# Two-layer streaming encoder: the body of the expert loop holds four experts in place of two

## What is computed

```
def swiglu(h, wg, wu, wd):
    return (jax.nn.silu(h @ wg) * (h @ wu)) @ wd
...
    logits = (h @ p['router'][j]).astype(jnp.float32)
    top_v, top_i = lax.top_k(logits, TOP_K)
    gates = jax.nn.softmax(top_v, axis=-1)
    w_e = jnp.einsum('btk,btke->bte', gates, jax.nn.one_hot(top_i, N_EXPERTS, dtype=jnp.float32))
    for e in range(N_EXPERTS):
        out = out + w_e[..., e:e + 1] * swiglu(h, p['e_gate'][j, e], p['e_up'][j, e], p['e_down'][j, e]).astype(jnp.float32)
```

## Time and profile before

| | |
|---|---|
| median of 3 runs | 2176.72 us (2172.87 to 2177.47) |
| the profiled execution: time | 2173.31 us |
| the profiled execution: span of the trace | 2171.5 us |
| PE busy | 2080.8 us (96%) |
| DVE busy | 1413.3 us (65%) |
| ACT busy | 1021.1 us (47%) |
| granted PE clock, mean | 0.97 |
| expert stage | about 1100 us to the end |

### The profile page before, as it was taken

How to read it: one execution, slowest core, us unless ns; L and a number is a source line. 1 busy time by engine, 2 the same in 40 slices (tenths; PEclk the granted TensorE clock), 3 DMA queues, 4 the chain that set the end, 5 groups by cost and what they waited for, 6 DMA issues and landing times.

```text
span 2171.5 us, 27716 instructions
## 1 busy us (share of the span) xinstructions
PE 2080.8 (96%) x10564; PEld 1688.0 (78%) x10564; DVE 1413.3 (65%) x1736; ACT 1021.1 (47%) x1168; POOL 140.4 (6%) x108
## 2 busy tenths in 40 slices
PE   7999998899999999997899999999999999999998
PEld 5767685699997777785778888888887888888886
DVE  1445633377772447433368787978878788797887
ACT  1333311143332334211256666766666666676765
POOL 2000000154430000000000000000000000000000
PEclk9999998999999999998889999999999999999999
DMA  7312210424443322110469897988979889898895
GB/s 278 123 64 117 88 48 17 161 101 162 174 161 119 120 106 88 59 59 17 154 227 341 320 343 299 360 321 336 344 268 356 322 335 344 305 353 327 330 349 214
DMA packets 61584, 467.41 MB, mean 215 GB/s; under 512 B 7592, under 2 KB 7848, under 8 KB 9744
## 3 DMA queue, kind: packets, MB, share of 16 engines
q1 hardware_dynamic: 58896, 459.86, 56.0%
q0 software_dynamic: 2560, 5.85, 0.8%
HBM read 462.66 MB, written 3.02 MB: 214 GB/s over the span
## 4 chain that ended last, share of the span: by engine, by line
PE 92%; DVE 5%; ACT 2%; issue 1%; POOL 0%; DMA 0%; DVEq 0%; ACTq 0%; POOLq 0%
PE ps L501 12%; PE ps L946 10%; PE ps L951 10%; PE ps L948 9%; PE ps L646 8%; PE ps L971 5%; PE ps L977 5%; PE ps L972 5%; PE ps L922 4%; PE ps L665 3%; PE ps L842 2%; PE ps L846 2%; PE ps L849 2%; PE ps L959 1%; PE ps L865 1%; PE ps L866 1%
## 5 line engine op out<-in xcount | busy, mean ns | idle before, releaser
L1871 DVE TENSOR_TENSOR ring_r<-ring,unit_hi 128x2048 fp32r<-128x2048 f32 x288 | 653.0, 2290 | 134.2 <-ACT unit_hi L1355 131.9
L1355 ACT ACTIVATE unit_hi<-ring 128x2048 fp32r<-128x2048 f32 x288 | 542.6, 1913 | 3.4 <-issue 3.4
L946 PE MATMUL ps<-unit_hi,hg_hi 128*128 128x512 f32 x896 | 251.2, 402 | 2.3 <-issue 2.3
L948 PE MATMUL ps<-unit_hi,hg_lo 128*128 128x512 f32 x896 | 242.2, 392 | 0.0
L646 PE MATMUL ps<-h,ring 128*128 128x288 f32 x768 | 217.8, 423 | 1.7 <-ACT arena L1188 1.0
L501 PE MATMUL ps<-h,ring 128*128 128x288 f32 x832 | 208.6, 413 | 9.5 <-DVE h L1463 9.5
L951 PE MATMUL ps<-ring_r,hg_hi 128*128 128x512 f32 x772 | 212.3, 397 | 1.4 <-issue 1.4
L501 PEld LDWEIGHTS ps<-h,ring 128*128 128x128 f32 x832 | 160.4, 193 | 56.1 <-issue 11.4
L948 PEld LDWEIGHTS ps<-unit_hi,hg_lo 128*128 128x128 f32 x896 | 169.3, 189 | 37.2
L946 PEld LDWEIGHTS ps<-unit_hi,hg_hi 128*128 128x128 f32 x896 | 160.7, 189 | 34.2 <-issue 2.8
L971 PE MATMUL ps<-unit_hi,h_e_hi 128*128 128x512 f32 x448 | 178.2, 398 | 3.2 <-DVE h_e_lo L1886 3.2
(11 more groups left out here) (383 smaller groups left out, 2889.1 us busy)
## 6 DMA issues: line engine op xcount, KB each, us to landing
ring<-in_w_exp SPq DMA_DIRECT2D x288, 1024.0 KB, 4.8
ring<-in_w_mix SPq DMA_DIRECT2D x44, 1536.0 KB, 6.6
unit<-in_w_exp SPq DMA_DIRECT2D x48, 1024.0 KB, 4.8
ring<-in_w_ffn SPq DMA_DIRECT2D x22, 1536.0 KB, 6.3
rel_table<-rel_row POOLq DMA_DIRECT2D x8, 256.0 KB, 8.9
const<-in_const SPq DMA_DIRECT2D x1, 1186.0 KB, 8.6
x<-in_xT SPq DMA_DIRECT2D x1, 1152.0 KB, 5.1
out_yT<-x SPq DMA_DIRECT2D x4, 288.0 KB, 2.2
```

Of the source, the lines that this page charges most:

```text
L946: mm(out, hg_hi[:, hp, 4 * w + k, :], hi[:, 512 * k:512 * k + 512], start=(w == 0 and k == 0), stop=False)
L948: mm(out, hg_lo[:, hp, 4 * w + k, :], hi[:, 512 * k:512 * k + 512], start=False, stop=False)
L1355: fn(unit_hi(q), unit(q), ACT.Copy).then_inc(s["uhi_made"], 1)
L1871: v.tensor_tensor(unit_lo(q), unit(q), unit_hi(q).bitcast(F32), ALU.subtract).then_inc(s["ulo_made"], 1)
```

## The change

On PE, ACT and DVE the loop advances by two, and its body holds `it2` and `then2 = it2 + 1`, four experts. `final - 1` is even for all three values of `final`, so the loop covers the same numbers: 1 to 2, 1 to 6 or 1 to 10. SP, POOL, the data and the order of the work are as they were.

```
-                with pe.Fori(1, final) as it2:
+                with pe.Fori(1, pe.snap(final - 1), 2) as it2:
                     expert(it2, 0, False, False)
                     expert(it2, 1, False, False)
+                    then2 = pe.snap(it2 + 1)
+                    expert(then2, 0, False, False)
+                    expert(then2, 1, False, False)
                 expert(final, 0, False, False)
                 expert(final, 1, False, True)
```

More of the change, by code:

```diff
@@ L1406, in experts @@
                 final = act.value_load(npass[0:1, 1:2], min_val=3, max_val=11)
-                with act.Fori(1, final) as it2:
+                with act.Fori(1, act.snap(final - 1), 2) as it2:
                     expert(it2, 0, False, False)
                     expert(it2, 1, False, False)
+                    then2 = act.snap(it2 + 1)
+                    expert(then2, 0, False, False)
+                    expert(then2, 1, False, False)
                 expert(final, 0, False, False)
@@ L1940, in experts @@
                 final = dve.value_load(npass[0:1, 1:2], min_val=3, max_val=11)
-                with dve.Fori(1, final) as it2:
+                with dve.Fori(1, dve.snap(final - 1), 2) as it2:
                     expert(it2, 0, False, False)
                     expert(it2, 1, False, False)
+                    then2 = dve.snap(it2 + 1)
+                    expert(then2, 0, False, False)
+                    expert(then2, 1, False, False)
                 expert(final, 0, False, False)
```

## The result

| | before | the change |
|---|---|---|
| median | 2177.98 us (6 runs, 2172.87 to 2179.73) | 2168.36 us (6 runs, 2163.38 to 2170.01) |
| ratio | | 0.9956, 95% interval 0.9942 to 0.9970 |
| profiled execution: time, span | 2173.31, 2171.5 us | 2169.02, 2167.2 us |
| PE's instruction packets (q8), all | 80 | 78 |

The change is faster by 0.44% (0.30 to 0.58%), 9.6 us between the medians. The predicted 2171.2 us is 2.8 us too high, and the gain at 5.48 us too small by the medians. A second measurement of the same kernel (experiment 6) gave 0.9954 (0.9942 to 0.9966).

A forecast was written before the change was run, and what follows sets the result against it. PE was taken to bound the kernel, stalled only at its one expert-loop back-edge: -5.48 us there, 0 for the new branch, SP's loads and longer body, so 2176.72 - 5.48 = 2171.2 us, range 2166.5 to 2175.0.

The forecast's parts named there:

- What bounds, and where: Expert stage: PE, 96% busy, sets the end; its only idle times, 2.3 and 1.4 us, lie at the back-edge.
- The price: PE's back-edge between experts 3 and 4: removing it frees 5.48 us, from select distances 138.65 and 133.17.
- the forecast's own median: Whole kernel: 2171.2 us, from before's median 2176.72 less 5.48, carrying over 3.4 us between median and profiled execution.
- ACT and DVE: Their back-edges must go too; with PE's alone removed, PE would wait about 4.7 us for DVE's `h_e_lo`, queued behind ACT.
- the forecast of 4.7: Near the back-edge: PE's wait in us for `h_e_lo` if PE alone lost its stall, 5.48 less 0.76 spare.
- SP and the loads: SP keeps its loop; its loads still arrive in time, cost 0, thinnest spare 1.0 us, units behind gaining on ACT.
- Rival B: At SP's loads: PE's stall hid them, so ACT would wait without it; 2173 to 2175 us, chance 0.07.
- The longer body: Four-expert loop body: the same instructions pass each engine but for the branch, so it costs 0 us.
- Rival C: New code of the longer body: refills stop PE, 8 x 1.42 = 11.4 less 5.48, +5.9 us, 2182.6; chance 0.05.
- Rival A: At the back-edge: it isn't what costs, or the stall only moves; no change, 2176.7 us, chance 0.11.
- its smaller version: At the back-edge: second issue wait and slow clock hang on something else, only 2.32 us goes; 2174.4 us.

The follow-up runs named there:

- experiment 6: The changed kernel, unedited, measured once more; ratio 0.9954 (0.9942 to 0.9966) to before, median 2168.57 us.
- experiment 11: The kernel before, unedited, run a third time for its trace; ratio 1.0000 (0.9990 to 1.0009).
- experiment 2: Kernel before with four experts in PE's loop body alone, ACT and DVE keeping two; ratio 0.9992 (0.9981 to 1.0003) to before.
- experiment 10: Kernel before with four experts in PE's and ACT's loop bodies, DVE keeping two; ratio 0.9993 (0.9983 to 1.0002) to before.
- experiment 3: Kernel before with four experts in ACT's and DVE's loop bodies, PE keeping two; ratio 1.0004 (0.9993 to 1.0016) to before.
- experiment 4: The changed kernel with SP's loop over pairs of experts written out too; ratio 0.9964 (0.9951 to 0.9977) to before, median 2167.66 us.
- experiment 5: Kernel before with the loop turned by one expert on PE, ACT and DVE, giving two back-edges; ratio 0.9973 (0.9963 to 0.9983) to before.
- experiment 1: The kernel before, unedited, run once more; ratio 1.0002 (0.9993 to 1.0011), 9.31 us for the back-edge.
- experiment 7: Kernel of experiment 3 with PE's code shifted by 48 wait instructions at the start; ratio 0.9977 (0.9967 to 0.9987) to before.
- experiment 8: Kernel of experiment 3 with PE's code shifted by 128 wait instructions at the start; ratio 1.0009 (1.0000 to 1.0019) to before.
- experiment 9: Kernel before, its back-edge kept on PE, ACT and DVE, with SP's loop written out; ratio 0.9989 (0.9979 to 0.9999) to before.

## Why the prediction was right, and where it was off

**What bounds, and where.** Right. The only PE waits of the stage were those of the back-edge, and with it gone there are none: every distance is 133.1 to 133.2 us in the change, twice.

**The price.** This step was mis-sized. The term was 5.48 us, "because it is measured over a whole expert". It is, but in one execution, and the price varies: 5.48 in the first trace, 9.31 and 9.33 in the two others, with q8 fetching two pieces at once (1637.00 and 1637.13 in experiment 11) and a granted clock of 0.57 in 1640 to 1652 us in both, where the first trace had 0.86. The 105 runs of before and twelve of the change put the gain at 8.0 us by the medians and 8.8 by the means. An estimate from 5.5 and 9.3 makes 66% of the executions the dear kind by the medians and 87% by the means; two traces of three were. That there are just two values isn't shown: the runs of before spread from 2172 to 2180 us without a gap. That the direction held doesn't hang on this, as the cheap form already gains 5.5 us. Which form the one trace read had was chance: with 9.31 us the same sum would have given 2167.4. The same may show in the forecast's own median: the 3.4 us by which the profiled execution lay below the median were carried over as a constant, but the two executions of the dear kind took 3.1 and 2.5 us more than it (2176.38 and 2175.83 against 2173.31). So for the most part they may have been this price, and would then go with the back-edge. Taking the profiled time as the base, with its own price, would have given 2167.8, nearer to the 2168.4 measured.

**ACT and DVE.** Right that PE alone gains nothing (5.9 us remain, experiment 2; the forecast of 4.7 lacked the half clock after the wait). The reading of DVE was incomplete: the prediction saw it as queued behind ACT, and experiment 10 shows a refill of its own, worth 5.1 us. Each of those tested costs most of it by itself, 5.7 for PE (3), 5.9 for ACT with DVE (2), 5.1 for DVE (10), and together 5.5 to 9.3; ACT alone wasn't run. PE's 5.7 is from a trace with a lone packet; a dear form of it, as in experiment 1, isn't ruled out. They overlap, so they can't be added, and neither PE's alone (2), nor ACT's and DVE's (3), nor PE's and ACT's (10) was worth removing without the rest.

**SP and the loads.** Right in that it costs nothing. SP's pause stays, from 1620.22 to 1628.20 in the change's trace, and the next units come in time:

```profile
1620.22 0.33 SPq L353 DMA_DIRECT2D ring<-in_w_exp  x1
...
1628.20 3.71 SPq L353 DMA_DIRECT2D ring<-in_w_exp  x4
```

1628.20 + 4.8 = 1633.0, and ACT takes that unit at 1634.67: 1.7 us of spare. But the units behind don't gain on it at once, as the prediction expected them to. The unit issued at 1637.31 lands at 1646.85 in the trace and ACT takes it at 1647.81: 0.96 us, the thinnest of all. Rival B didn't come in the change, and with SP's pause removed nothing more is gained that can be told (experiment 4). It stood near, though. In experiment 5 the second unit behind SP's pause took 8.1 us from issue to landing, where the change's took 6.6, and ACT did wait for units, with no effect seen in the distances (ACT's waits, 1120 to 2150 us):

```profile
ACT unit_hi L1353 <- DMA ring<-in_w_exp: 0.5, 2, 0.3
```

**The longer body.** Right at 0. Rival C is out: q8 has 6 packets in 1638 to 1777 us in the change, and PE waits at none of them. That is 2 fewer than the 8 of before, which the prediction read against the 4 of the stretch ahead; its 4 was low, since the next packet came at 1638.22, just behind the edge. Rival A is out by the distances; its smaller version too. The 108 ns that the Trainium skill gives for a compare-and-branch (Advanced Engine Details and Errata, section Control Flow Timing) isn't what the traces show across this one: 5.5 to 9.3 us lie there, for the refill.

## What to carry to other kernels

A back-edge whose target must be brought in again costs a refill on each engine concerned, and these refills lie side by side: here it paid to remove all three, and not one or two. Compare equal stretches on either side of it, as the selects here, and do it in more than one trace, since the price can vary between executions. Look at the queues of kind instruction too, as a refill can stand in the profile as a wait for another engine (experiments 3, 5 and 10). Where the body can't be made longer, turning the loop or shifting its code is worth a try: the same work with two back-edges ran 0.27% faster than with one.

## What the runs showed of the hardware

- The price of one back-edge with a body of two experts ranged from 1.46 us (experiment 5, where only PE refills, with no half clock) to 9.3 us (before, two packets at once).
- With a lone packet, PE's next matmul came 2.5 to 2.8 us after q8's packet started, in the first trace of before and in experiments 3, 5, 7, 8 and 9. PE's first wait ranged from 1.2 to 2.6 us all the same, since the packet started from 1.46 us before PE ran out of matmuls (9) to 0.04 after (7). What sets that lead is left open.
- A refill's second piece doesn't follow the first at once: q8's second packet starts 5.6 to 5.9 us after the first in the first trace of before and in experiments 3, 5, 7, 8 and 9. Before, 3 and 9 wait for it; with the code shifted by 48 or 128 instructions PE has no second wait. That the head of the loop then stands further from the end of a piece is the reading that the shifts were chosen by.
- Ahead of the experts, in code that no experiment touched but for its place, the first select falls at 1152.6 to 1155.1 us in ten of the traces and at 1149.0 to 1149.5 in three (5, 7 and 10). In 640 to 900 us the granted clock is 0.95 in before and 0.97 in experiment 5, at the same PE busy time per window but 33 matmuls more. Experiment 8 has this faster form too (1195 matmuls, 0.97), hidden behind its pads (before first, then experiment 5):

```profile
640.00:900.00 260.00, 244.77 (x1164) 186.72 (x1163) 127.96 (x259) 81.44 (x169) 5.19 (x9) 0.95 0.28 104
```

```profile
640.00:900.00 260.00, 244.78 (x1197) 187.84 (x1196) 128.62 (x260) 82.26 (x170) 5.18 (x9) 0.97 0.30 111
```

Such a difference of 3 to 6 us between traces is as large as the effect studied, and is a further reason to read distances. What starts it is left open.
